# Mixture-of-experts stage: experts in an order set by their loads, two slot groups instead of three for three of them, down weights in pairs of rows

## The reference

```python
logits = xt @ w_router                        # 256 x 8
top_logit, top_idx = lax.top_k(logits, 2)
gates = softmax(top_logit)
# for each chosen expert e of a row:
y = (silu(x @ w_gate[e]) * (x @ w_up[e])) @ w_down[e]   # 1024 -> 3584 -> 1024
out[row] += gate * y
```

## Time and profile before

| | |
|---|---|
| median of three runs | 1425.06 us |
| span of the profiled execution | 1422.2 us |
| what lies around the span | 2.9 us, taken as the difference of the two |
| instructions | 33237 |

### The profile page before, as it was taken

How to read it: one execution, slowest core, us unless ns; L and a number is a source line. 1 busy time by engine, 2 the same in 40 slices (tenths; PEclk the granted TensorE clock), 3 DMA queues, 4 the chain that set the end, 5 groups by cost and what they waited for, 6 DMA issues and landing times.

```text
span 1422.2 us, 33237 instructions
## 1 busy us (share of the span) xinstructions
PE 1394.8 (98%) x15137; PEld 833.4 (59%) x15137; DVE 441.0 (31%) x748; ACT 328.8 (23%) x528; POOL 29.7 (2%) x42
## 2 busy tenths in 40 slices
PE   6999999999999999999999999999999999999997
PEld 6987888888899853453453353353354354344344
DVE  4656655655686742101101101101101101101102
ACT  4645545445566531000000000000000000000001
POOL 2000000000012100000000000000000000000000
PEclk9999999999999999999999999999999999999998
DMA  9734555556443489999999999999999999999980
GB/s 296 252 119 146 195 177 194 191 180 198 149 120 140 148 332 326 401 419 389 391 418 387 392 417 389 394 415 393 388 414 400 392 405 402 393 402 408 393 332 32
DMA packets 133041, 438.42 MB, mean 308 GB/s; under 512 B 10690, under 2 KB 64160, under 8 KB 116512
## 3 DMA queue, kind: packets, MB, share of 16 engines
q1 hardware_dynamic: 131824, 433.26, 80.1%
q0 software_dynamic: 1072, 2.98, 0.7%
HBM read 435.16 MB, written 1.05 MB: 307 GB/s over the span
## 4 chain that ended last, share of the span: by engine, by line
PE 95%; DVE 3%; DMA 1%; issue 0%; ACT 0%; POOL 0%; SPq 0%; DVEq 0%
PE bank L1366 41%; PE bank L1387 20%; PE bank L1131 6%; PE bank L881 6%; PE bank L883 6%; PE bank L882 6%; PE bank L1132 4%; PE bank L1134 1%; PE bank L1415 1%; PE bank L1435 1%; DMA raw<-in_ev_w_in 1%; DVE arena L2142 0%; PE bank L1003 0%; PE bank L1049 0%; POOL arena L1849 0%
## 5 line engine op out<-in xcount | busy, mean ns | idle before, releaser
L1366 PE MATMUL bank<-ring,arena 128*32 128x512 f32 (+1 forms) x6144 | 583.5, 540 | 0.0
L1366 PEld LDWEIGHTS bank<-ring,arena 128*32 128x32 f32 x6144 | 197.7, 110 | 365.2 <-issue 362.5
L1387 PE MATMUL bank<-ring,arena 128*32 128x256 f32 x5376 | 291.5, 379 | 0.0
L1387 PEld LDWEIGHTS bank<-ring,arena 128*32 128x32 f32 x5376 | 175.1, 110 | 116.7 <-issue 3.1
L679 DVE TENSOR_TENSOR low<-raw,high 128x2048 fp32r<-128x2048 f32 x73 | 167.3, 2294 | 85.1 <-ACT high L674 84.9
L674 ACT ACTIVATE high<-raw 128x2048 fp32r<-128x2048 f32 x73 | 139.3, 1910 | 55.8 <-PE bank L883 44.1
L1131 PE MATMUL bank<-ht_both,high 128*128 128x512 f32 x392 | 140.5, 398 | 0.6 <-DVE ht_both L1901 0.6
L2413 DVE TENSOR_TENSOR expert_rows<-expert_rows,bank 128x512 f32<-128x512 f32 (+1 forms) x48 | 29.8, 621 | 344.3 <-issue 217.3
L1788 ACT ACTIVATE expert_rows<-bank 128x512 f32<-128x512 f32 (+1 forms) x48 | 25.9, 544 | 422.9 <-PE bank L1366 422.9
L1132 PE MATMUL bank<-ht_both,low 128*128 128x256 f32 x448 | 116.8, 281 | 0.0
L1799 ACT ACTIVATE y_h<-bank 128x256 fp32r<-128x256 f32 x24 | 9.2, 383 | 403.9 <-PE bank L1387 403.9
(11 more groups left out here) (316 smaller groups left out, 1206.8 us busy)
## 6 DMA issues: line engine op xcount, KB each, us to landing
ring<-in_moe_w_down SPq DMA_DIRECT2D x112, 1024.0 KB, 8.4
ring<-in_moe_w_gate SPq DMA_DIRECT2D x64, 1024.0 KB, 9.1
ring<-in_moe_w_up SPq DMA_DIRECT2D x64, 1024.0 KB, 8.6
ring<-in_moe_w_gate SPq DMA_DIRECT2D x64, 768.0 KB, 5.9
ring<-in_moe_w_up SPq DMA_DIRECT2D x64, 768.0 KB, 6.6
raw<-in_ffn_w_gate SPq DMA_DIRECT2D x14, 1024.0 KB, 5.0
raw<-in_ffn_w_up SPq DMA_DIRECT2D x14, 1024.0 KB, 5.0
raw<-in_ffn_w_down SPq DMA_DIRECT2D x14, 1024.0 KB, 5.0
```

Of the source, the lines that this page charges most:

```text
L1366: ins = mm(ps(use)[q * GRP:(q + 1) * GRP, 0:width], rows[:, k, r * GRP:(r + 1) * GRP], weights[:, q, :, :], start=k == 0, stop=k == DK - 1)
L1387: ins = mm(ps(use)[q * GRP:(q + 1) * GRP, 0:DN], m_act_t[:, r, first + c, :], ring[:, at + c * DM + q * DN:at + c * DM + (q + 1) * DN], st ...
```

## The change

1. **Order by load.** The program now fixes the number of groups of each item, 3, 2, 3, 3, 2, 3, 2, 3 (`ITEM_GROUPS`), not its expert. VectorE ranks the loads at run time: expert 0 is always item 0, the three smallest loads of the others are items 1, 4 and 6, which have two groups (64 rows), and the rest are items 2, 3, 5 and 7. The slot and gate tables are permuted into item order, TensorE's `counts` is done ahead of `rank`, and SyncE reads the next item's expert from a table (`order_i`) once per item and addresses its weights by that register. A load over 64 in an item of two groups gets a further item.
2. **Two groups.** All loops over groups (`expert_gate_up`, `expert_down`, `combine`, `gate_silu`, `gated`, `down_low`, `turned_selection`) run over `groups(item)`. `plan_banks` lays out every item by itself, since the counts differ; the up products move to banks 5, 4, 3 from 3, 4, 5.
3. **Pairs of rows.** In a down piece partition p holds the neighbouring rows 2p and 2p+1 of the piece, one run of 8 KB, instead of rows p and p+128. The weight columns that gate and up multiply are picked in runs of 64 instead of 32, and VectorE's turn of the activation reads every second column, so that the inner indices match.

```diff
+ITEM_GROUPS = (3, 2, 3, 3, 2, 3, 2, 3)
+N_SMALL = ITEM_GROUPS.count(NG - 1)
+FIRST_SMALL = NE - N_SMALL
...
+    c[:, C_PLACE:C_PLACE + NE] = ITEM_PLACE
+    c[:, C_KEY:C_KEY + NE] = np.where(np.arange(NE) == 0, 1e6, -np.arange(NE))
...
+def groups(item):
+    return range(ITEM_GROUPS[item] if item < NE else NG)
+def down_order(item):
+    return [r for r in DOWN_ORDER if r in groups(item)]
...
-                banks.fill(("mu", part, r), NG + r, NQ)
+                banks.fill(("mu", part, r, item), 2 * NG - 1 - r, NQ)
...
-                    return dst.rearrange("p (k f) -> p k f", k=2), columns(wt, 0, first, first + 2, DM)
+                    rows = wt[first * P:(first + 2) * P, :].rearrange("(p k) c -> p k c", k=2)
+                    return dst.rearrange("p (k f) -> p k f", k=2), rows
...
             def later_turns(item, expert):
                 wt = {kind: expert_weights(kind, expert) for kind in "gud"}
+                following = None
                 for j in range(FIRST_TURN, EXPERT_PIECES):
                     wait_expert_used(sp, held_before(j), item)
                     load_expert(wt, j)
+                    if j == 2 * FIRST_TURN and item + 1 < NE:
+                        if item == 0:
+                            sp.wait_ge(order_ready, 1)
+                        following = sp.value_load(order_i[0:1, item + 1:item + 2], min_val=0, max_val=NE - 1)
+                return following
...
+            expert = 0
             for item in range(NE):
-                later_turns(item, item)
+                expert = later_turns(item, expert)
                 if item + 1 < NE:
-                    first_turn(item + 1, item)
+                    first_turn(expert, item)
...
             pe.wait_ge(rsel_ready, 1)
+            for t in range(T):
+                last = mm(ps("counts")[:, 0:NE], ones, r_sel[:, t, :], start=t == 0, stop=t == T - 1)
+            last.then_inc(fill_sem("counts"), 1)
             rk = ps("rank")
...
-            for t in range(T):
-                last = mm(ps("counts")[:, 0:NE], ones, r_sel[:, t, :], start=t == 0, stop=t == T - 1)
-            last.then_inc(fill_sem("counts"), 1)
...
-                weights = ring[:, at:at + NQ * width].rearrange("p (b q i) -> p q b i", q=NQ, i=GRP)
+                weights = ring[:, at:at + NQ * width].rearrange("p (b q i) -> p q b i", q=NQ, i=2 * GRP)
...
-                for r in range(NG):
-                    use = ("m" + kind, part, r)
+                for r in groups(item):
+                    use = ("m" + kind, part, r, item)
...
-                                r_slot[:, t, items, None].to_broadcast([P, FIRST_ITEMS, SLOTS]),
+                                r_slot_i[:, t, items, None].to_broadcast([P, FIRST_ITEMS, SLOTS]),
...
+            def in_item_order(out, by_expert):
+                moved = r_cmp.rearrange("p (t i) e -> p t i e", t=T)
+                steps.done(V.tensor_tensor(moved, by_expert[:, :, None, :].to_broadcast([P, T, NE, NE]),
+                                           item_of[:, None, :, :].to_broadcast([P, T, NE, NE]), ALU.mult))
+                return V.tensor_reduce(out.rearrange("p t i -> p (t i)"), r_cmp, AX, ALU.add)
             dve.wait_ge(rsel_ready, 1)
+            dve.wait_ge(*filled("counts"))
+            steps.done(V.scalar_tensor_tensor(r_key, ps("counts")[:, 0:NE], float(NE), cst[:, C_KEY:C_KEY + NE], ALU.mult,
+                                              ALU.add))
+            n = steps.mark(V.tensor_tensor(keys_above, r_key[:, None, :].to_broadcast([P, NE, NE]),
+                                           r_key[:, :, None].to_broadcast([P, NE, NE]), ALU.is_gt))
             dve.wait_ge(*filled("rank"))
             V.tensor_tensor(r_slot, ps("rank")[:, 0:T * NE].rearrange("p (t e) -> p t e", t=T), r_sel,
                             ALU.mult).then_inc(drain_sem("rank"), 1)
+            steps.wait(n)
+            steps.done(V.tensor_reduce(r_place, keys_above, AX, ALU.add))
+            steps.done(V.tensor_tensor(item_of, r_place[:, None, :].to_broadcast([P, NE, NE]),
+                                       cst[:, C_PLACE:C_PLACE + NE, None].to_broadcast([P, NE, NE]), ALU.is_equal))
             dve.wait_ge(*drained("rank"))
+            steps.done(in_item_order(r_slot_i, r_slot))
             one_hot_first(0, 0)
...
+            steps.done(in_item_order(r_slot_i, r_gate))
...
+            V.tensor_copy(order_i[0:1, :], r_place[0:1, :]).then_inc(order_ready, 1)
...
-                for r in range(NG):
-                    dve.wait_ge(*drained(("mu", part, r), item))
-                    V.transpose(m_act_t[:, r, first:first + blocks, :].rearrange("p b c -> p (b c)"),
-                                m_act[:, r, 0:width]).then_inc(turned_ready, 1)
+                for r in groups(item):
+                    dve.wait_ge(*drained(("mu", part, r, item)))
+                    V.transpose(m_act_t[:, r, first:first + blocks, :].rearrange("p (b c) s -> p b c s", c=2),
+                                m_act[:, r, 0:width].rearrange("p (b i c) -> p b c i", i=GRP, c=2)).then_inc(
+                                    turned_ready, 1)
```

More of the change, by code:

```diff
@@ L57 @@
 NITEM = NE + NOVER
+ITEM_GROUPS = (3, 2, 3, 3, 2, 3, 2, 3)
+N_SMALL = ITEM_GROUPS.count(NG - 1)
+FIRST_SMALL = NE - N_SMALL
+ITEM_PLACE = tuple(sum(g == group for g in ITEM_GROUPS[:n]) + (FIRST_SMALL if group < NG else 0)
+                   for n, group in enumerate(ITEM_GROUPS))
+assert len(ITEM_GROUPS) == NE and ITEM_GROUPS[0] == ITEM_GROUPS[-1] == NG and set(ITEM_GROUPS) <= {NG - 1, NG}
 NEXTRA = NOVER + 1
@@ L269, with groups_before @@
 DOWN_ORDER = (2, 0, 1)
+Y_FIRST = 4 * NG
+def groups(item):
+    return range(ITEM_GROUPS[item] if item < NE else NG)
+def down_order(item):
+    return [r for r in DOWN_ORDER if r in groups(item)]
+def groups_before(item):
+    return sum(len(groups(i)) for i in range(item))
 DOWN_BANKS = {0: 6, 1: 7, 2: 2}
@@ L648, in first_halves, with product @@
             return [piece(buf, 0, DK)[:, 4 * i:4 * i + 4, :] for i in range(2)]
-        def product(key):
+        def product(key, item):
             kind, part, _ = key
-            return ("md", DOWN_ORDER[-1]) if kind == "d" else ("m" + kind, part, NG - 1)
+            return ("md", DOWN_ORDER[-1], item) if kind == "d" else ("m" + kind, part, groups(item)[-1], item)
         def expert_landed(j, item):
@@ L660, in wait_expert_used @@
             if ends_a_product(key):
-                eng.wait_ge(*filled(product(key), item))
+                eng.wait_ge(*filled(product(key, item)))
             else:
                 pieces = len(EXPERT_COUNTED) * item + EXPERT_COUNTED.index(key) + 1
-                if not isinstance(item, int):
-                    pieces = nc.sync.snap(pieces)
                 for q in range(NQ):
@@ L1781, in gate_silu @@
             def gate_silu(part, item):
-                for r in range(NG):
-                    use = ("mg", part, r)
-                    act.wait_ge(*filled(use, item))
+                for r in groups(item):
+                    use = ("mg", part, r, item)
+                    act.wait_ge(*filled(use))
                     if part:
-                        act.wait_ge(*drained(("mu", 0, r), item))
+                        act.wait_ge(*drained(("mu", 0, r, item)))
                     fn(m_silu[:, r, 0:WIDTHS[part]], ps(use)[:, 0:WIDTHS[part]], ACT.Silu).then_inc(drain_sem(use), 1)
@@ L2255, in turned_selection @@
             def turned_selection(item):
-                dve.wait_ge(*filled("sgt", item))
-                for r in range(NG):
-                    last = V.tensor_scalar(sgt[:, r, :], ps("sgt")[:, 0:SEQ], cst[:, C_SLOTP + r:C_SLOTP + r + 1], None,
+                use = ("sgt", item)
+                dve.wait_ge(*filled(use))
+                for r in groups(item):
+                    last = V.tensor_scalar(sgt[:, r, :], ps(use)[:, 0:SEQ], cst[:, C_SLOTP + r:C_SLOTP + r + 1], None,
                                            ALU.is_equal)
-                last.then_inc(drain_sem("sgt"), 1)
+                last.then_inc(drain_sem(use), 1)
             def one_hot_extra(item):
```

151 lines of the change are left out of this document (84 added, 67 removed).

## The result

The changed kernel takes 1379.46 us (median of 4 runs, 1378.22 to 1380.19), the kernel before 1424.72 us beside it (4 runs). The ratio is 0.9683, 95% interval 0.9668 to 0.9698: 45.3 us less, where 56 were forecast. The profiled execution took 1379.12 us, its span is 1377.3 us.

A forecast was written before the change was run, and what follows sets the result against it. PE bounds the kernel; after the change, loads do from item 1. Last piece lands at 1344.8, item 7 ends at 1352.9; plus 12.0 to the span's end, 1.6 routing, 2.9 around the span: 1369 us, range 1358 to 1397 (own 1358 to 1383).

The forecast's parts named there:

- The mechanism: Expert stage: 108.7 us of PE work go, loads set the pace from item 1 on, and 56 us are gained.
- The strongest rival: Expert loads: 768 KB pieces stay at 373 GB/s and down pieces at 409, giving 1397 us; chance 0.18.
- The pairs: Down pieces: 8 KB runs raise the rate from 409 to 419 GB/s, 6.0 us over seven experts.
- the pairs do nothing: Rival on down pieces: their rate stays at 409 GB/s despite longer runs, giving 1375 us; chance 0.06.
- The slower rival: Small items: waits drop TensorE's clock to 1.2 GHz and it stays there, giving 1542 us; chance 0.06, of which 0.02 half-way.
- The rate: Expert loads from item 1 on: 419 GB/s, 105.1 us per expert, 709.5 us for the 297.3 MB left.
- Routing: Ahead of the first gather: two steps of 0.33 us and four of 0.24 add 1.6 us to the end.
- The fall of the clock: Routing: PE's clock might fall for 3.4 us while it idles, 1.7 us more; not taken into the forecast.
- Item 7: Last item, three groups: starts with its first piece at 1242.2, takes 110.7 us on PE, ends at 1352.9.
- Around the span: Outside the profiled span: 2.9 us, from 1425.06 less 1422.2, added to the span of 1366.5.
- A full ring: Sign of a wrong forecast: a full ring in items 2 and 3 would mean PE is still the bound.
- SyncE's issue: SyncE's added register loads and addressing: cost 0, as an issue takes 0.33 us against 2.5 us for a piece.

The follow-up runs named there:

- Experiment 1: The changed kernel with one group instead of two in items 1, 4 and 6, loads unchanged: 1377.37 us, ratio 0.9665 to the kernel before.
- experiment 4: The changed kernel with three groups in every item, keeping the new order, routing steps and pairs: 1429.24 us, ratio 1.0033 to the kernel before.
- After: The changed kernel itself, with all three parts of the change: 1379.46 us, ratio 0.9683 to the kernel before.
- experiment 8: The changed kernel with SyncE waiting, before each ring load, for the fourth piece before to land: 1378.63 us, ratio 0.9671 to the kernel before.
- experiment 5: The changed kernel with seven unused matmuls of 128 columns between the rank sums and the first gather: 1375.83 us, ratio 0.9663 to the kernel before.

## Why the prediction was right, and by how much it missed

**The mechanism held.** PE gives up 108.7 us and the loads take over from item 1 on: items 2 and 7 begin at a landing, PE waits for ring loads in items 1, 4 and 6, landings grow to 21 to 27 us, the rate has no dips. Experiment 1 shows that the loads set the end, experiment 4 that the order alone gains nothing.

**The rate of the small pieces.** The strongest rival, with 0.18, had 768 KB pieces at 373 GB/s even with a full queue. After shows 410 to 421 in every slice of 18 us but the last, with those pieces in each expert: the dips of the earlier trace rows came from PE's spacing, as the short landings said. A DMA share of 0.99 at 373 did not speak for a limit.

**The pairs.** 6.0 us forecast; 5.6 by the medians, 6.0 by the ratios, 6.6 from the same point. That the result, 1379.5, lies nearer to the 1375 of "the pairs do nothing" than to 1369 is chance: this rival did not come, and the miss has another cause.

**The clock.** The slower rival did not come: 1.00 through items 1, 4 and 6. The Trainium skill (TensorE: Matmul & The Clock Gate, section "HAM oscillation — how this bites in real kernels") tells of waits for DMAs that let the clock fall before every burst; with two groups the trace does not show it, with one group it does (0.50 from 967 to 973 us), but without a loss, as the loads were late anyway.

**Where the 10 us are.** Against the profiled execution, 1379.1 us, the forecast of 1369.4 was 9.7 short. By its own steps:

| step | forecast | measured | us |
|---|---|---|---|
| item 0 ends (forecast 635.3 + 1.6) | 636.9 | 639.86 | +2.9 |
| from there to item 7's first piece | 606.9 | 614.9 | +8.0 |
| item 7 on PE | 110.7 | 110.5 | -0.2 |
| last down product to the end of the span | 12.0 | 12.0 | 0 |
| around the span | 2.9 | 1.8 | -1.1 |

- *The rate is the term that was mis-sized.* "At 419 GB/s an expert takes 105.1 us" was read from a backlog of 24 us, which the prediction called a long window. From item 2's first landing (722.34) to item 7's (1254.80) five experts of 44.04 MB landed in 532.46 us: 413.6 GB/s, 106.5 us per expert. The moved rate was 418; 1.7 of it were not weights, and part of the rest was lead, which experiment 8 shows to be worth nothing: there 413.6 GB/s of weights moved, and the end was the same. Moved bytes over 24 us show neither. The estimate by the Trainium skill (HBM Reference, section Specifications (TRN2), where the prediction says Access), 699.5 us for the same bytes, was further off: they took 719.3.
- *Routing:* 1.6 us forecast for the steps; experiment 5 gives 1.4, so this held. The fall of the clock was named with up to 1.7 us more and not taken; it came, and cost 1.4 to 1.5 in the profiled execution of after and 2.2 to 2.5 in five others. The reason against it, that PE had kept the clock when idle by a third, looked at the wrong stretch: ahead of the gathers PE is now busy for 1.11 of 3 us. Of the 2.9 in the table 1.4 are this fall, and most of the rest, 1.6, lies ahead of L1383 (509.12 against 507.56 before), in stages that the change doesn't touch.
- *Item 7:* the forecast hung its end on the last landing plus 8.1 us, and the last landing came 6.1 us before it. The step itself, first piece plus 110.7 us, held.
- *Around the span* the forecast put 2.9 us, one set's median less the span of one execution. Every run on record lies about 1.8 us above its own span. This error of 1.1 us goes the other way, so that it made the miss look smaller by luck.
- *A full ring* in items 2 and 3 was named as a sign that PE is still the bound, and SyncE did wait 37 us for places there (722 to 944 us). But pieces landed 25 us after their issue, so that the ring was held largely by pieces still under way, and the rate stayed at 418 to 419 GB/s. The sign was badly chosen; the time to landing tells the two cases apart.
- *SyncE's issue* was priced at 0.33 us. With after's long queue a gate piece's takes 1.9 us in the median and up to 6.2. With four in flight it is 0.33 again and the time is the same, so the longer issue costs nothing: 0, as forecast.

## What to carry to other kernels

Where two resources are both near full, work the end out from bytes at the other one's rate before counting what is saved on the first: of the 108.7 us saved here, 63 became waiting or new cost. The rate for that should come from how fast pieces land over a long stretch, not from what moves in a short backlog. Once the loads bound, work is worth removing only where it holds loads back (the full ring of item 0) or stands behind the last one (item 7), and longer runs pay only there, behind a full queue.

## What the runs showed of the hardware that was not expected

- The DMA engines seem not to keep step: after 700 us of one stream the last 17 us run at a mean share of 0.50 and 206 GB/s, and with four pieces in flight at 0.91 and 378. Per busy engine the rate is the same (206 / 0.50 = 412), so those still at work don't gain from the others' rest.
- A DMA issue holds SyncE longer when the queue is long. After's issues of gate pieces (duration in ns, least, median, longest; first and last start), against 332 to 337 ns for the last nine issues in experiment 8:

```profile
L811 SPq DMA_DIRECT2D ring<-in_moe_w_gate x128: 327/1856/6207, 453.3 to 1286.4; - x128
```

- Behind a gap of some 1.95 us on TensorE, in a stretch with PE busy for 1.11 of 3 us, the clock fell to 0.50, in all seven profiled kernels that have the gap; seven small matmuls in it kept the clock at 1.00 in both that have them.
